# mLSTM stage: values with tokens on partitions beside a column of ones, no division, running maximum spread once a head

## What is computed

```
D[t,s]   = exp(b[t] - b[s] + i[s] - m[t])  for s <= t, else 0
score    = (q[t] . k[s]) / 8 * D[t,s]
num[t]   = sum_s score * v[s]         den[t] = sum_s score
h[t]     = num[t] / max(|den[t]|, exp(-m[t]))
h        = h * rsqrt(mean over the head's 128 features of h^2 + 1e-6) * norm_g
```

## Time and profile before

| | |
|---|---|
| median of 3 runs | 3076.71 us (3071.97 to 3077.7) |
| the profiled execution | 3072.38 us |
| its span | 3070.6 us |
| mean granted clock of TensorE | 0.938 |
| TensorE busy | 2739.9 us, 89% |
| VectorE, ScalarE, GpSimd busy | 43%, 23%, 49% |
| matrix products of the mLSTM stage | from 1952.37 us on |

### The profile page before, as it was taken

One profiled execution on the slowest core, in us unless ns is written; L12 is line 12 of the kernel. 1 busy time (PEld: TensorE's weight loads), 2 busy tenths in 40 slices (PEclk: granted clock), 3 DMA queues, 4 the chain that ended last, 5 costly groups with the idle time before them and its releaser, 6 DMA issues. The chain is left out here.

```text
span 3070.6 us, 33335 instructions
## 1 busy us (share of the span) xinstructions
PE 2739.9 (89%) x11900; PEld 2119.2 (69%) x11900; DVE 1325.3 (43%) x1853; ACT 705.8 (23%) x976; POOL 1503.3 (49%) x1022
## 2 busy tenths in 40 slices
PE   5896779999988997889988989978997989899997
PEld 4783457888857774668947857647875668678774
DVE  4954333212249997637013225242064313454352
ACT  2003642000143343220032023242022220210002
POOL 2443015666638884457415725305651156466651
PEclk7997889999999998899999999999999999999998
DMA  7531002333212221122121212102330032223220
GB/s 249 188 101 62 1 14 68 96 97 101 100 46 82 82 82 55 58 69 96 55 69 55 96 42 83 55 0 57 98 93 28 14 96 69 69 94 95 85 77 36
DMA packets 230473, 231.17 MB, mean 75 GB/s; under 512 B 9995, under 2 KB 228844, under 8 KB 230252
## 3 DMA queue, kind: packets, MB, share of 16 engines
q1 hardware_dynamic: 225968, 228.74, 23.6%
q10 hardware_dynamic: 4412, 1.24, 0.2%
HBM read 227.86 MB, written 2.10 MB: 75 GB/s over the span
## 5 line engine op out<-in xcount | busy, mean ns | idle before, releaser
L829 POOL TENSOR_SCALAR Wh<-raw 128x2048 fp32r<-128x2048 f32 (+3 forms) x197 | 367.0, 1864 | 1416.4 <-PE PS L873 1177.6
L835 POOL TENSOR_TENSOR Wl<-raw,Wh 128x512 fp32r<-128x512 f32 (+3 forms) x772 | 1027.4, 1363 | 29.1 <-issue 1.6
L873 PE MATMUL PS<-Hh,Wh 128*128 128x512 f32 (+2 forms) x2104 | 841.7, 400 | 121.7 <-DVE Hl L596 55.9
L873 PE MATMUL PS<-Hl,Wh 128*128 128x512 f32 (+2 forms) x2104 | 835.3, 397 | 0.0
L873 PE MATMUL PS<-Hh,Wl 128*128 128x512 f32 (+2 forms) x2104 | 834.3, 397 | 0.0
L873 PEld LDWEIGHTS PS<-Hh,Wh 128*128 128x128 f32 (+2 forms) x2104 | 401.9, 191 | 233.8 <-issue 94.9
L873 PEld LDWEIGHTS PS<-Hh,Wl 128*128 128x128 f32 (+2 forms) x2104 | 401.2, 191 | 90.9 <-issue 1.5
L873 PEld LDWEIGHTS PS<-Hl,Wh 128*128 128x128 f32 (+2 forms) x2104 | 402.3, 191 | 86.1
L873 PE MATMUL PS<-Bh,Wh 128*128 128x512 f32 x688 | 271.9, 395 | 17.8 <-DVE Bl L1784 9.1
L873 PE MATMUL PS<-Bl,Wh 128*128 128x512 f32 x688 | 270.4, 393 | 0.0
L873 PE MATMUL PS<-Bh,Wl 128*128 128x512 f32 x688 | 270.4, 393 | 0.0
(11 more groups left out here) (305 smaller groups left out, 2979.0 us busy)
## 6 DMA issues: line engine op xcount, KB each, us to landing
raw<-in_w_in SPq DMA_DIRECT2D x44, 1024.0 KB, 5.7
raw<-in_w_ff SPq DMA_DIRECT2D x32, 1024.0 KB, 5.3
raw<-in_conv_w_in SPq DMA_DIRECT2D x24, 1024.0 KB, 5.1
raw<-in_ret_w_in SPq DMA_DIRECT2D x24, 1024.0 KB, 5.2
spare<-in_ada_w SPq DMA_DIRECT2D x20, 1024.0 KB, 6.7
raw<-in_w_up SPq DMA_DIRECT2D x20, 1024.0 KB, 5.3
raw<-in_w_out SPq DMA_DIRECT2D x8, 1024.0 KB, 5.2
raw<-in_conv_w_out SPq DMA_DIRECT2D x8, 1024.0 KB, 5.2
```

The source lines that it names most:

```text
L829: pool.tensor_scalar(st.Wh[0:rows, slot, k, 0:g.width], st.raw_slot(slot)[0:rows, k, 0:g.width], 1.0, 1.0, ALU.mult, ALU.mult)
L835: ins = pool.tensor_tensor(st.Wl[0:rows, slot, k, 0:g.width], st.raw_slot(slot)[0:rows, k, 0:g.width], st.Wh[0:rows, slot, k, 0:g.width].b ...
L873: mm = pe.matmul(out, lhs, rhs, start=(k == 0 and n == 0), stop=(k == parts[-1][0] and n == 2))
```

## The change

- Values: W is now the stationary operand (128 keys x 128 tokens) and V the moving one, with a column of ones beside the 128 features: numerators and denominator come out with tokens on partitions, in ten products of 129 columns a head (q blocks of tokens, b up to q). V is stored as 129 columns per block and head, so it reaches one tile further, and the heads' outputs O begin at tile 17, not 16.
- The running maximum is spread once a head, for all 512 tokens (`spread_floor`, two products), and a head ahead. The causal mask is no longer added before the exponential: VectorE cuts the diagonal block afterwards (min with 1, times a matrix of 0 and 1).
- The floor is turned into columns beside g_i, and no longer spread.
- Numerators are copied from PSUM by VectorE (`keep`), with the denominator times 1e-3. ScalarE squares each block of 128 features with an accumulated sum. For groups of four heads, VectorE adds mean square and the squared larger of denominator and floor (times 1e-6), ScalarE takes Ln and Exp(-0.5 x) on 16 columns, VectorE scales, TensorE turns the head back to features on partitions (fp32 transposes), and ScalarE copies it out with norm_g as scale.

The diff, without removed lines that stand above in full:

```diff
+def heads_with_one(st):
+    flat = st.A[:, 8:17, :].rearrange("p c n -> p (c n)")
+    return flat[:, 0:NB * M_HEADS * (P + 1)].rearrange("p (b h n) -> p b h n", b=NB, h=M_HEADS)
+def to_heads(st):
+    def act(e, acc, i, p):
+        return e.activation(heads_with_one(st)[:, :, ds(i * 4 + 2 * p, 2), 0:P],
+                            acc.rearrange("p b (h a n) -> p (b h) a n", h=2, a=2), ACT.Copy)
...
@@ gates_parts, rest.vector
-        dve.memset(st.Bh[:, 0:4, :].bitcast(F32), 0.0)
+        dve.memset(st.Bh[:, 0:2, :].bitcast(F32), 0.0)
+        dve.memset(heads_with_one(st)[:, :, :, P], 1.0)
...
@@ gates_parts, rest.tensor
+        pe.wait_ge(floor_in, 1)
+        for n, rows in enumerate((g_i, floor)):
+            for b in range(NB):
+                at = (n * NB + b) * M_HEADS
+                mm = pe.transpose(st.PS[:, 6, at:at + M_HEADS], rows[:, b * P:(b + 1) * P], st.ident[hs, hs])
...
@@ mlstm_part, tensor (score loses its spread and mask)
+        def spread_floor(h):
+            if h >= 2:
+                pe.wait_ge(exped, NB * (h - 1))
             for half_of in range(2):
+                mm = pe.matmul(st.PS[:, 2 + h % 2, :], pick(h), negM[:, half_of, :], start=(half_of == 0),
+                               stop=(half_of == 1))
+            mm.then_inc(spread, 1)
         def values(h):
             if h:
+                pe.wait_ge(kept, h)
+            pe.wait_ge(weighted, NB * (h + 1))
+            for q in range(NB):
+                for b in range(q + 1):
+                    mm = pe.matmul(num[:, q // 2, q % 2, :], W(h, b)[:, q * P:(q + 1) * P], V[:, b, h, :],
+                                   start=(b == 0), stop=(b == q))
+            mm.then_inc(pv_done, 1)
+        def turn(h):
+            pe.wait_ge(scaled, h + 1)
+            if h >= 2:
+                pe.wait_ge(head_out, h - 1)
+            for q in range(NB):
+                mm = pe.transpose(st.PS[:, 6 + h % 2, q * P:(q + 1) * P], O(h)[:, q * P:(q + 1) * P], st.ident)
+            mm.then_inc(turned, 1)
+        spread_floor(0)
+        for h in range(M_HEADS):
             for b in range(NB):
+                score(h, b)
+                if b == 0 and h + 1 < M_HEADS:
+                    spread_floor(h + 1)
+                if b == 1 and h:
+                    values(h - 1)
+                if h == M_HEADS - 1 and b:
+                    turn(b - 1)
+        values(M_HEADS - 1)
+        for h in range(GROUP - 1, M_HEADS):
+            turn(h)
@@ mlstm_part, scalar
+        def squares(h):
+            act.wait_ge(kept, h + 1)
+            if h >= 2:
+                act.wait_ge(squared, h - 1)
+            for q in range(NB):
+                ins = act.activation(SQ(h, q), O(h)[:, q * P:(q + 1) * P], ACT.Square,
+                                     accum_out=SS[:, NB * h + q:NB * h + q + 1])
+            ins.then_inc(squared, 1)
+        def rstd(g):
+            act.wait_ge(measured, g + 1)
+            act.activation(group(LN, g), group(LN, g), ACT.Ln)
             act.drain()
+            act.activation(group(R, g), group(LN, g), ACT.Exp, scale=-0.5).then_inc(rstd_in, 1)
+        def out(h):
+            act.wait_ge(turned, h + 1)
+            act.activation(O(h), st.PS[:, 6 + h % 2, :], ACT.Copy,
+                           scale=col(st, "m_norm_g_3", h)).then_inc(head_out, 1)
+        for h in range(M_HEADS):
+            for b in range(NB):
+                act.wait_ge(spread, h + 1)
+                if h >= 2:
+                    act.wait_ge(pv_done, h - 1)
+                act.activation(W(h, b)[:, at(b)], st.PS[:, 2 + h % 2, at(b)], ACT.Exp,
+                               bias=st.cols[:, 16 * b + h:16 * b + h + 1]).then_inc(exped, 1)
+                if h == GROUP + 1 and b == 1:
+                    rstd(0)
+                if h == M_HEADS - 1 and b >= 2:
+                    out(b - 2)
             if h:
+                squares(h - 1)
+        squares(M_HEADS - 1)
+        rstd(1)
+        for h in range(2, M_HEADS):
+            out(h)
@@ mlstm_part, vector
+        def keep(h):
+            dve.wait_ge(pv_done, h + 1)
+            dve.tensor_copy(O(h).rearrange("p (c a n) -> p c a n", c=2, a=2), num[:, :, :, 0:P])
+            cols = slice(NB * h, NB * h + NB)
+            dve.tensor_scalar(T[:, cols].rearrange("p (c a) -> p c a", c=2), num[:, :, :, P], 1e-3, None, ALU.mult)
+            dve.drain().then_inc(kept, 1)
...
+        def scale(h):
+            dve.wait_ge(rstd_in, h // GROUP + 1)
+            for q in range(NB):
+                o = O(h)[:, q * P:(q + 1) * P]
+                ins = dve.tensor_scalar(o, o, R[:, NB * h + q:NB * h + q + 1], None, ALU.mult)
+            ins.then_inc(scaled, 1)
...
+        def cut(h, b):
+            dve.wait_ge(exped, NB * h + b + 1)
+            w = W(h, b)[:, b * P:(b + 1) * P]
+            dve.scalar_tensor_tensor(w, w, 1.0, causal, ALU.min, ALU.mult)
+        for h in range(M_HEADS):
+            if h == GROUP + 1:
+                measure(0)
+            cut(h, 0)
             for b in range(NB):
+                n = NB * h + b
+                if b + 1 < NB:
+                    cut(h, b + 1)
                 dve.drain()
+                dve.wait_ge(scored, n + 1)
+                dve.scalar_tensor_tensor(W(h, b)[:, at(b)], st.PS[:, n % 2, at(b)], 0.125, W(h, b)[:, at(b)],
+                                         ALU.mult, ALU.mult).then_inc(weighted, 1)
+                if b == 1 and h:
+                    keep(h - 1)
+                if h == GROUP + 2:
+                    scale(b)
+        keep(M_HEADS - 1)
+        measure(1)
+        for h in range(GROUP, M_HEADS):
+            scale(h)
```

More of the change, by code:

```diff
@@ L1447, in mlstm_part @@
     ctx = ExitStack()
-    (scored, spread, exped, weighted, pv_done, floor_in, absed, divided, squared, ss_in, rstd_in, head_out) = sems(
-        nc, ctx, "ml", "scored spread exped weighted pv floor absed divided squared ss rstd head_out")
-    V = st.A[:, 8:16, :].rearrange("p (b c) n -> p b (c n)", b=NB)
+    (scored, spread, exped, weighted, pv_done, kept, squared, measured, rstd_in, scaled, turned, head_out) = sems(
+        nc, ctx, "ml", "scored spread exped weighted pv kept squared measured rstd scaled turned head_out")
+    V = heads_with_one(st)
     W = lambda h, b: st.spare[:, 4 + 8 * (h % 2) + b, :]
-    negM, floor = (st.Bh[:, k:k + 2, :] for k in (0, 2))
-    R, T, SQ, LN = (st.A[:, c, :] for c in (25, 26, 27, 31))
+    O = lambda h: st.A[:, 17 + h, :]
+    negM = st.Bh[:, 0:2, :]
+    SQ = lambda h, q: st.A[:, 25 + 2 * (h % 2), q * P:(q + 1) * P]
+    table = lambda k: st.A[:, 26, 32 * k:32 * k + 32]
+    SS, T, LN, R, FLOOR = (table(k) for k in range(5))
     at = lambda b: slice(b * P, S)
     pick = lambda h: st.ident_r[:, h:h + 1].to_broadcast([P, P])
+    num = st.PS[:, 4:6, 0:2 * (P + 1)].rearrange("p c (a n) -> p c a n", a=2)
+    GROUP = 4
+    group = lambda a, g: a[:, NB * GROUP * g:NB * GROUP * (g + 1)]
     part = Part(ctx)
@@ L1477, in values @@
         def values(h):
             if h:
[L1479 to L1483, removed]
-            for b in range(NB):
[L1485 to L1501, removed]
+                pe.wait_ge(kept, h)
[4 more added lines that the diff above has]
+                                   start=(b == 0), stop=(b == q))
@@ L1517, in _ @@
[L1517 to L1524, removed]
-                    act.activation(W(h, b)[:, at(b)], st.PS[:, 2 + (NB * h + b) % 2, at(b)], ACT.Exp,
-                                   bias=st.cols[:, 16 * b + h:16 * b + h + 1]).then_inc(exped, 1)
-                if b == 1 and 1 <= h <= M_HEADS:
-                    act.wait_ge(pv_done, h)
-                    if h >= 2:
-                        act.wait_ge(divided, h - 1)
-                    act.activation(T, st.PS[:, 5, :], ACT.Abs).then_inc(absed, 1)
-            if h >= 2:
-                tail2(h - 2)
+        def squares(h):
[6 more added lines that the diff above has]
+            ins.then_inc(squared, 1)
@@ new lines, in _ @@
+        dve.tensor_tensor(FLOOR, FLOOR, FLOOR, ALU.mult)
+        dve.drain()
+        causal = st.A[:, 28, 0:P]
+        dve.tensor_tensor(causal, st.sq["strict"], st.ident, ALU.add)
+        dve.drain()
+        def cut(h, b):
[6 more added lines that the diff above has]
+            cut(h, 0)
+            for b in range(NB):
+                n = NB * h + b
+                if b + 1 < NB:
+                    cut(h, b + 1)
+                dve.drain()
+                dve.wait_ge(scored, n + 1)
[5 more added lines that the diff above has]
+                    scale(b)
```

64 lines of the change are left out of this document (16 added, 48 removed).

## The result

The changed kernel takes **3019.45 us** (median of 4 runs, 3014.1 to 3026.64), the kernel before 3075.16 beside it; the ratio is 0.9831, with a 95% interval of 0.9812 to 0.985. The forecast was 3020. That agreement hides two errors: in the profiles the stage costs more than I said, and what stands behind it costs less.

What follows compares the result with a forecast made beforehand. TensorE, busy 89% of the span, was taken as the bound, waiting in the mLSTM stage's 13.55 us heads. Stage 68.2 + 5.3 for clock = 73.5 us, gain 56.4: 3016, plus 4.3 to the median, 3020 us; range 3009 to 3037.

Steps and rivals of the forecast that it cites:

- The stage as the only place: mLSTM stage, 129.9 us: nothing is prepared meanwhile for later, so every microsecond saved there is one of the kernel.
- the chain before: Waits over one old head, through VectorE's maximum, reciprocal, product and TensorE's products: repeats each 13.55 us.
- The chain after: Waits over one changed head, through scores, spread, values, copy, cut and third weighing: 6.7 us where it was 13.55.
- The second ring: Copy, squares, exponentials, cut and weighings of a head: 5.4 us, at upper ends 6.5, so it does not bind.
- The head with the two table loads: Head 5, two loads and two small ACTIVATEs between exponentials: 3.1 us, slack hides 1.9, so +1.2.
- The clock: TensorE at 1.2 GHz after the stage's start, +4 us, and in the last turnings, +1.3.
- The signs: In the changed profile: heads 6.5 to 7 us, values 0.22 to 0.23 apart, five table loads, mid-stage clock 1.0.
- the first: Rival: each of 15 links of a head's two rings takes 0.1 us more, cycle 8.2, total 3031; chance 0.15 with what lies between.
- The second: Rival: TensorE stays at 1.2 GHz, a head takes 5 us more, stage some 105, total 3052; chance 0.05.
- The third: Rival: weight loads of the values' products are exposed, about 18 us a head, stage 160, total 3107; slower, chance 0.02.
- The fourth: Rival: another wait, such as W's two buffers, replaces the reciprocal; 11 us a head, gain 22, total 3055; chance 0.04.
- Table loads at 1.30 and not 2.66: ScalarE's table loads priced by the trace; an added 1.38 drain would cost up to 5.5 us more, total 3026.

Runs made afterwards that it cites:

- fillers and PSUM: Changed kernel plus products nobody reads in TensorE's waits and the cuts' 0/1 matrix in PSUM for heads 0 to 6: 3003.6 us, ratio 0.9785 to the kernel before.

## Why the prediction was right, and where not

- **The stage as the only place, and the chain before**: right. Removing the row sums took off exactly their time from a head, removing the table loads next to nothing (1.4 us of stage).
- **The chain after**: right, link by link, 6.81 us for a forecast of 6.7. The second ring had its slack, as the table loads put back show. The head with the two table loads took 7.47 (copies at 1999.73 and 2007.20) for 7.9; there the prediction lets slack hide 1.9 us where its own two rings, 6.7 and 5.4, leave 1.3, and it still forecast too much. The tail from the last copy, 2032.25 to 2043.06, took 10.8 us for 10.7 and 1.3 of clock. The cuts' price of 0.29 holds but beside GpSimd, where it was up to 1.41; that term is worth 0.7 us of the stage. With clock 1.00 and that cause gone (fillers and PSUM) the whole stage takes 69.4 us, for a sum of 68.2.
- **The clock**: the wrong step, a term of the sum that was mis-sized. "In some 10 us TensorE's 5.5 of a head become about 10, so +4; the last turnings +1.3" was 5.3 in the sum and measured 10 and 17 in the two profiles (77.8 and 85.3, less 68.2). In the second it was an affair of start and end after all, but a dearer one: up to the second copy 24.9 us passed for a forecast of 17.5 (10.8 and 6.7), and 8.7 for 6.7 in the sixth interval is most of the rest. In the first the clock fell in the middle too, which I had ruled out because the middle of the old stage had 0.98 at 79% busy: a full-clock head of the new stage has TensorE busy for 5.90 of 6.81 us, 87%, and still there were stretches of 6 us at 0.50. The busy share did not tell. Fillers take the low clock away; what causes it stays open.
- **The signs**: five table loads came, the values 0.24 us apart, and no product waited for its weights. But heads came over 8 us apart (four in the first execution, two in the second), which I had named as a sign of being wrong, and the clock in the middle was 1.0 in one of two executions.
- **The rivals**: the first (links 0.1 us longer each) did not happen. The second, 1.2 GHz throughout, holds for a third to a half of the stage, and with a reciprocal more for two thirds. The third is out: its loads are hidden, 2.44 us for ten products with ten different weights on all 128 rows. The Trainium skill's sentence in "TensorE: Matmul & The Clock Gate", section "The mechanism", that loads overlap with running products only where the row group differs, does not hold in this trace, and the measurement decides. The fourth is out: no head at full clock but the one with the table loads takes over 6.81 us.
- **Table loads at 1.30 and not 2.66**: right. The timeline of the changed kernel at the end of the stage:

```profile
2033.38 0.29 ACT L1539 ACTIVATE A<-A 128x128 f32<-128x128 f32 x1
2033.58 0.19 ACT L1539 ACTIVATION_READ_ACCUMULATOR A<-A 128x1 f32 x1
2033.67 0.29 ACT L1539 ACTIVATE A<-A 128x128 f32<-128x128 f32 x1
...
2034.37 1.28 ACT L1545 ACT_TABLE_LOAD   x1
...
2035.66 0.22 ACT L1545 ACTIVATE A<-A 128x16 f32<-128x16 f32 x1
```

  The load begins at 2034.37 and its ACTIVATE at 2035.66. That is 1.29 us; the drain of 1.38 on top, from the section of the Trainium skill that the prediction names ("ScalarE: Activation LUTs", "What ACT_TABLE_LOAD costs"), is not borne out here either. The squares before it go 0.29 apart, where I took 0.36.
- **The total**: the forecast of 3020 came from a stage of 73.5 us. In the profiles it was 78 to 85, and the median still fell by 55.7. The products behind the stage make up for part: in the four profiles with the old stage (before, and three with a thing out of it) the part behind took 983.0 to 989.5 us, in the ten with the new one 980.4 to 984.0. I did not forecast that, and no run isolates it. A part of it arises at once: ScalarE's first copy comes 14.2 us behind the stage's end in the profile before (13.1 to 14.2 in the four), and 12.8 in the profile after; where the rest arises the runs do not settle. And the part ahead of the stage varies by 14 us from one execution to the next. So that 3019.45 met 3020 is luck in part: too small a clock term, a gain behind the stage that I had not seen, and executions that differ by more than either.

## What to carry to other kernels

Before pricing a removed wait, ask what stands right behind it: the reciprocal was worth 2.4 us a head alone, and the whole chain 6.7 once TensorE's own work in a head shrank with it, from 11.2 us to 5.9. Where TensorE waits a little in every round, look at the granted clock per stretch and not at the busy share: here work off TensorE in its chain cost twice its length, and rounded products written to a free bank in those waits brought the clock back for 0.15 us a head. Fill no more than the wait, or the fillers become the pace. Work that is needed soon but not now (here the next head's spread) belongs in such a wait rather than on the chain.

## What the runs showed of the hardware

- The granted clock fell to 1.2 GHz with no wait of TensorE inside the heads above 2.0 us (changed kernel), and even after 39 us at 2.4 GHz in which TensorE was busy for 38.2 us and never waited longer than 0.2 us (kernel before without the reciprocal). With the waits filled its mean over the stage was 1.00, 1.00, 0.97 and 0.97 in four executions. It differs between executions of one kernel: 0.76 and 0.85.
- Ten fp32 products of 129 columns with ten different weights took 2.44 us at full clock, their twenty weight loads hidden.
- A VectorE operation with two SBUF operands lasted up to 1.41 us in place of 0.29 while GpSimd worked, and 0.29 with one operand in PSUM. The Trainium skill has this in "SBUF — State Buffer", under its terms: VectorE and GpSimd share a pair of ports, held by one for a whole instruction. The trace agrees: the long cut ends 0.15 us after the GpSimd operation that it began beside.
- Square with an accumulator on 128 columns goes at 0.29 us start to start (fence above), the read of 0.19 between them hidden; four with their reads take 1.28.
